# Low-rank rows opened in the projections, first units side by side, the norm's root ahead of the middle work

## The chip, the cores and the metric

The kernel runs on one core of one Trainium2 chip. The metric is the device time of one execution in microseconds (us), the median of several runs. Lower is better.

## The reference

Two transformer blocks follow one another, over 1024 tokens of width 1024, all in float32. Cut to what matters here:

```python
# first block
h = rmsnorm(x, norm_mix);  proj = h @ w_in            # 51 tiles of 128 columns
y_a = retention(rq, rk, rv, rg) @ w_ret_o
y_b = nsa(q, kc, vc, ks, vs, kw, vw, gates) @ w_nsa_o
x = x + (sigmoid(ga) * y_a + sigmoid(gb) * y_b) @ w_out
x = x + conv_ffn(rmsnorm(x, norm_ffn));  x = rmsnorm(x) * norm_final
# second block (ada = silu(c) @ w_ada + b_ada gives shifts, scales and gates)
z, u = split(modulate(rms_norm(x)) @ w_in_2)           # 14 tiles of z, 4 of u
z = z + mu_shift * (z_prev - z)
r, k, v, w_lo, a_lo, g_lo = split(z)                   # 4, 4, 4, 1/2, 1/2, 1 tiles
decay = exp(-exp(-softplus(-(w0 + tanh(w_lo) @ w2)) - 0.5))
a = sigmoid(a0 + a_lo @ a2);  g = sigmoid(g_lo) @ g2
y = rwkv7 recurrence(r, decay, k, v, -kk, kk * a) * g
x = x + gate * concat(y, s5(u)) @ w_out_2
x = x + gate * (silu(h @ w_gate) * (h @ w_up)) @ w_down   # h = modulate(rms_norm(x))
out = rms_norm(x) * final_gain
```

## The kernel before, in words

Activations stay in on-chip memory with the features on the 128 partitions: `xT` is x, `hi` and `lo` are the two parts of the normed x (eight tiles of 128x1024 each). A product `w.T @ h` is made in three passes (high weight by high, high weight by low, low weight by high), so a **unit**, 128 output rows over 1024 tokens, is 8 k tiles times 3 passes times 2 halves = 48 matmuls of 128x512. Weights come by DMA on SP's queue into one of two buffers, are split in two parts (`pool_high` at L192 and a subtraction) and used while the next is loaded. A unit's buffer is split anew for unit u+2 only once unit u's products are done (`products_done`, or `up_done` in the feed-forward), and TensorE starts unit u+2 when that split is done and the accumulator has been read.

The program is a row of stages, each a block of its own per engine with a barrier between (`phase`, L75 and L72). Within a stage every engine runs its list in the order written; waits are on semaphores. `rms_programs` (L294) makes a norm: ACT squares (where no sums are there yet), PE sums over partitions (L343), DVE takes mean and reciprocal (L333, L334), then ACT runs `act_middle`, then the root (L316) and the row's copy (L318), PE spreads the row (L350), and DVE, ACT and POOL make tile after tile of `mid` (L391 or L393), `hi` (L384) and `lo` (L404). In the two feed-forwards `act_middle` is `first_high` (L632: the high parts of the first two weights, which POOL then subtracts at L713); in the last norm it is `gain_too` (L529: four of the eight gains; DVE's scaling at L504 waits for them). `TwoNorms` in the second projections has no such middle work.

Four stages begin with such a norm: the first projections (product at L1409), the first feed-forward (L203), the second projections (L3430) and the second feed-forward (L203). There unit 0 waits at each k tile for that tile of `lo` (`norm.ready`), unit 1 comes whole after it:

```python
for u in range(N):                    # L1399, second projections alike
    for k in range(KD):
        if u == 0:
            norm.ready(pe, k)
```

After the first projections (with retention and compression in them) comes the retention's output product. `SplitTilesAndKeys` (L2005) gives its stage extra work: SP loads the raw keys (two of 64x2x1024, with 18 rows each beside them) and head 0's queries (82x1024), before it loads the stage's weights of units 1 and 2, since the norm's programs are written ahead of the product's. POOL loads two small constants, `edges` and `eye`, waits for both, and only then splits weights. POOL's DMAs go through another queue than SP's.

The second projections make units in the order u (4 tiles), then z tiles 0 to 12, with four S5 gate units in slots 17 to 20, then z tile 13. Tile 12 (`ZLO`) holds the low-rank rows of decay and rate, tile 13 (`ZG`) those of the gate. All z tiles go to DRAM (`proj2T`). The RWKV stage (L2421) then loads both, the low-rank weights `wa2` and `g2`, the chunk mask, the r, k and v of tile 0 and seven small tables on SP's queue; TensorE, ACT and POOL wait for all twelve constants (`CONSTS`), ACT makes tanh (L2944) and sigmoid (L2945) in place, and PE starts with `decay(0)` and `rate(0)` (L2513). ACT's `keys(0)` (L2840) comes behind both and needs the k tile.

## Time and profile before

| what | us |
|---|---|
| median of 3 runs (lowest to highest) | 3860.39 (3858.7 to 3864.57) |
| the profiled execution, its own time | 3864.79 |
| its span | 3863.0 |
| PE busy in the span | 3528.5 (91%) |
| DVE, POOL, ACT busy | 1776.0, 1030.7, 869.9 |

PE is TensorE's matmul sequencer, DVE VectorE, POOL GpSimd, ACT ScalarE, SP the queue that only issues DMAs. Times in rows are microseconds from the span's start. A name such as `ffn_whi` is a buffer of the kernel, its number left out. The granted clock is that of TensorE as a share of 2.4 GHz, so 0.50 is 1.2 GHz. The square brackets behind an instruction say how long its engine had been idle and what ended that. Rows of one instruction kind that follow each other closely are merged, with a count.

### The profile page before, as it was taken

To read this page: it belongs to the slowest core of one execution; us is meant where nothing else is said; L and a number is where in the kernel's file an instruction comes from. 1 tells how busy PE (TensorE), PEld (TensorE's weight loads), DVE (VectorE), ACT (ScalarE), POOL (GpSimd) and SP (SyncE) were. 2 spreads that over 40 slices of the span, in tenths; PEclk is the share of its full clock that TensorE was granted. 3 is DMA by queue.
4 is the path that set the end of the run, shared out by engine and by line. 5 is a ranking of instruction groups with operands and counts; after the bars stand their busy time and mean duration, and the time that the engine had idled before them with its cause. 6 is when DMAs were issued, how large, how long until landed. Compare 5 with 4: busy or idle time off the path is not lost. (4 is left out here: it accounts for less than half of the span.)

```text
span 3863.0 us, 55754 instructions
## 1 busy us (share of the span) xinstructions
PE 3528.5 (91%) x23230; PEld 2909.7 (75%) x23230; DVE 1776.0 (46%) x2725; ACT 869.9 (23%) x1260; POOL 1030.7 (27%) x491
## 2 busy tenths in 40 slices
PE   5999999989999898999999889959896899999997
PEld 4878777767777676888888767748784778888886
DVE  4762555423877734555555636134443322223233
ACT  2012122122434203111111220235431121111112
POOL 3332333333210234121212054122212332122221
PEclk7999999998999998999999989969997899999998
DMA  3453334333000312322222046221002111111111
GB/s 92 137 179 116 110 99 118 104 111 102 8 8 1 113 46 89 109 93 69 72 82 76 30 153 150 89 77 36 19 3 93 55 44 44 55 43 54 38 49 44
DMA packets 310711, 290.79 MB, mean 75 GB/s; under 512 B 21454, under 2 KB 276992, under 8 KB 309304
## 3 DMA queue, kind: packets, MB, share of 16 engines
q1 hardware_dynamic: 283738, 205.62, 18.2%
q10 hardware_dynamic: 26482, 82.06, 5.6%
q8 instruction: 153, 2.51, 0.3%
q0 software_dynamic: 288, 0.20, 0.1%
q14 instruction: 50, 0.41, 0.0%
HBM read 224.26 MB, written 63.57 MB: 75 GB/s over the span
## 5 line engine op out<-in xcount | busy, mean ns | idle before, releaser
L713 POOL TENSOR_TENSOR ffn_wlo<-ffn_raw,ffn_whi 128x1024 fp32r<-128x1024 f32 x88 | 211.4, 2404 | 1067.3 <-ACT ffn_whi L901 1012.9
L203 PE MATMUL up<-h_hi,ffn_whi 128*128 128x512 f32 x1408 | 439.6, 394 | 21.3 <-POOL h_lo L404 20.9
L203 PE MATMUL up<-h_lo,ffn_whi 128*128 128x512 f32 x1408 | 436.2, 391 | 0.0
L203 PE MATMUL up<-h_hi,ffn_wlo 128*128 128x512 f32 x1408 | 435.4, 390 | 0.0
L192 POOL TENSOR_TENSOR whi<-raw,ones 128x1024 fp32r<-128x1024 f32 (+1 forms) x83 | 155.3, 1872 | 754.9 <-PE acc L1409 460.9
L203 PEld LDWEIGHTS up<-h_hi,ffn_whi 128*128 128x128 f32 x1408 | 263.4, 189 | 79.2 <-POOL h_lo L404 14.4
L203 PEld LDWEIGHTS up<-h_lo,ffn_whi 128*128 128x128 f32 x1408 | 265.9, 189 | 56.2
L203 PEld LDWEIGHTS up<-h_hi,ffn_wlo 128*128 128x128 f32 x1408 | 265.7, 189 | 56.1
L1409 PE MATMUL acc<-h_hi,whi 128*128 128x512 f32 x816 | 273.6, 417 | 8.3 <-POOL h_lo L404 8.3
L804 DVE TENSOR_TENSOR ffn_prod<-ffn_act,up 128x1024 f32<-128x1024 f32 x44 | 53.8, 1222 | 465.6 <-PE up L203 460.8
L1409 PE MATMUL acc<-h_lo,whi 128*128 128x512 f32 x816 | 256.6, 396 | 0.0
L1409 PE MATMUL acc<-h_hi,wlo 128*128 128x512 f32 x816 | 254.5, 393 | 0.0
L901 ACT ACTIVATE ffn_whi<-ffn_raw 128x1024 fp32r<-128x1024 f32 x84 | 89.1, 1061 | 633.5 <-PE up L203 581.9
L203 PE MATMUL dn<-ffn_ghi,ffn_dhi 128*128 128x512 f32 x704 | 219.7, 394 | 7.9 <-issue 3.9
L203 PE MATMUL dn<-ffn_ghi,ffn_dlo 128*128 128x512 f32 x704 | 218.5, 392 | 0.0
L203 PE MATMUL dn<-ffn_glo,ffn_dhi 128*128 128x512 f32 x704 | 218.5, 392 | 0.0
L1409 PEld LDWEIGHTS acc<-h_lo,whi 128*128 128x128 f32 x816 | 156.2, 191 | 34.5
L1409 PEld LDWEIGHTS acc<-h_hi,wlo 128*128 128x128 f32 x816 | 155.2, 190 | 34.5
L1409 PEld LDWEIGHTS acc<-h_hi,whi 128*128 128x128 f32 x816 | 150.4, 193 | 39.3 <-issue 6.7
L835 DVE SCALAR_TENSOR_TENSOR xT<-dn,prm,xT 128x1024 f32<-128x1024 f32 x88 | 113.0, 1284 | 124.2 <-PE dn L203 124.2
L811 DVE TENSOR_TENSOR ffn_glo<-ffn_prod,ffn_ghi 128x1024 fp32r<-128x1024 f32 x44 | 139.5, 3170 | 56.7 <-ACT ffn_ghi L925 56.7
L833 DVE TENSOR_TENSOR xT<-xT,dn 128x1024 f32<-128x1024 f32 x88 | 107.4, 1221 | 123.1 <-PE dn L203 123.1
(549 smaller groups left out, 6635.7 us busy)
## 6 DMA issues: line engine op xcount, KB each, us to landing
raw<-w_in SPq DMA_DIRECT2D x51, 512.0 KB
projT<-proj_stage ACTq DMA_DIRECT2D x51, 512.0 KB, 2.7
ffn_ada_raw<-w_ada SPq DMA_DIRECT2D x24, 1024.0 KB, 5.0
ffn_raw<-w_up SPq DMA_DIRECT2D x44, 512.0 KB
ffn_draw<-w_down SPq DMA_DIRECT2D x11, 1024.0 KB, 6.9
ffn_raw<-ffn_w_gate SPq DMA_DIRECT2D x22, 512.0 KB
ffn_raw<-ffn_w_up SPq DMA_DIRECT2D x22, 512.0 KB
ffn_draw<-ffn_w_down SPq DMA_DIRECT2D x11, 1024.0 KB, 4.7
```

The lines of the kernel that those rows point to most:

```text
L192: return nc.gpsimd.tensor_tensor(out, x, one.unsqueeze(2).broadcast_to(x.shape), ALU.mult)
L203: last = nc.tensor.matmul(acc[:, t, :], w[:, k, w_cols], x[:, k, t * HALF:(t + 1) * HALF], start=(k == 0 and i == 0), stop=(k == k_tiles - ...
L713: nc.gpsimd.tensor_tensor(w_lo[i][:], raw[i][:], w_hi[i][:], ALU.subtract).then_inc(s[f"up_split{i}"], 1)
L804: nc.vector.tensor_tensor(prod[j][:].rearrange("p (h t) -> p h t", h=NH), act_out[:].rearrange("p (h t) -> p h t", h=NH), acc[1][:], ALU.m ...
L811: nc.vector.tensor_tensor(g_lo[:, j, :], prod[j][:], g_hi[:, j, :], ALU.subtract).then_inc(s["g_split"], 1)
L833: nc.vector.tensor_tensor(x, x, dn[b][:], ALU.add).then_inc(s[f"down_read{b}"], 1)
L835: nc.vector.scalar_tensor_tensor(out=x, in0=dn[b][:], scalar=prm[:, gate + n:gate + n + 1], in1=x, op0=ALU.mult, op1=ALU.add).then_inc(s[f ...
L901: nc.scalar.activation(w_hi[i][:], raw[i][:], ACT.Copy).then_inc(s[f"up_hi{i}"], 1)
L1409: last = nc.tensor.matmul(acc[b][:, t, :], w[:, k, :], x[:, k, t * HALF:(t + 1) * HALF], start=(k == 0 and i == 0), stop=(k == KD - 1 and ...
```

## The change

Five edits:

- In the four stages that begin with a norm, TensorE's first two units are made side by side: per k tile it waits once and makes 12 matmuls, six for each unit, in place of six. In the first projections the S5 parameters' transposes (`turn_params`), which stood inside unit 1, come after both units.
- In `rms_programs` the root and the row's copy come ahead of `act_middle`.
- The loads of keys and of head 0's queries go from SP's queue to POOL's, ahead of `edges` and `eye`.
- The second projections make `ZLO` and `ZG` in slots 4 and 5, into buffers that the RWKV stage keeps (`lora`, `glo`). ACT applies tanh and sigmoid in slots 6 and 7, behind those units' stores. Eight constants of the RWKV stage are loaded on SP's queue in the last slot.
- The RWKV stage loads only the chunk mask and `sel` (which count as its constants), then r, k and v. PE starts `decay(0)` at once and waits for the constants behind `norms_row(0)`; ACT's tanh and sigmoid and their wait are gone. `krow` has another address.

```diff
@@ rms_programs, ACT
-        if act_middle:
-            act_middle(act)
         act.wait_ge(s["norm_step"], 2)
         nc.scalar.activation(compact[:], compact[:], ACT.Sqrt).then_inc(s["root_done"], 1)
         act.wait_ge(s["root_turned"], 1)
         nc.scalar.activation(row[:], tot[0:NT, 1, 0:P], ACT.Copy).then_inc(s["row_done"], 1)
+        if act_middle:
+            act_middle(act)
@@ feed_forward, PE (both kinds)
+            def first_up_products():
+                for i in range(2):
+                    pe.wait_ge(s[f"up_split{i}"], 1)
+                for k in range(KD):
+                    norm.ready(pe, k)
+                    for i in range(2):
+                        last = tile_products(nc, acc[i], w_hi[i], w_lo[i], hi, lo, k, KD)
+                        if k == KD - 1:
+                            last.then_inc(s[f"up_done{i}"], 1)
...
-            up_products(0, 0)
+            first_up_products()
             up_products(0, 1)
@@ projections_and_retention, PE
+            for b in range(2):
+                pe.wait_ge(s[f"weight_split{b}"], 1)
+            for k in range(KD):
+                norm.ready(pe, k)
+                for b in range(2):
+                    last = tile_products(nc, acc[b], w_hi[b], w_lo[b], hi, lo, k, KD)
+                    if k == KD - 1:
+                        last.then_inc(s[f"products_done{b}"], 1)
+            turn_params()
+            for u in range(2, N):
@@ SplitTilesAndKeys.programs
-        @block.sync
-        def _(sp):
+        @block.gpsimd
+        def _(pool):
             for j, t in enumerate((KS, KW)):
                 k = projT[t * P:(t + 1) * P, :].rearrange("(g d) t -> d g t", d=NSA_D)
-                sp.dma_start(raw[j][low], k).then_inc(s["keys_in"], 16)
-                sp.dma_start(raw[j][NSA_D:rows], ins[("k_krows", "k_wrows")[j]]).then_inc(s["keys_in"], 16)
-            load_queries(nc, sp, N["qh"][0], projT, self.selT, ins, 0, s["query_in"])
-
-        @block.gpsimd
-        def _(pool):
+                pool.dma_start(raw[j][low], k).then_inc(s["keys_in"], 16)
+                pool.dma_start(raw[j][NSA_D:rows], ins[("k_krows", "k_wrows")[j]]).then_inc(s["keys_in"], 16)
+            load_queries(nc, pool, N["qh"][0], projT, self.selT, ins, 0, s["query_in"])
             pool.dma_start(N["edges"][:], ins["k_edges"]).then_inc(s["edges_in"], 16)
             pool.dma_start(N["eye"][:], ins["k_ident"]).then_inc(s["edges_in"], 16)
             pool.wait_ge(s["edges_in"], 32)
@@ projections2_and_s5
-    units = list(range(UU, N_PROJ2)) + list(range(UU))
+    units = list(range(UU, N_PROJ2)) + [ZLO, ZG] + list(range(ZLO))
+    opened = {ZLO: rw["lora"], ZG: rw["glo"]}
... SP
+                if u == N - 1:
+                    sp.wait_ge(s["gelu_done"], NG)
+                    load_rwkv_constants(sp, rw, ins, s["rw_consts"])
+                    sp.wait_ge(s["rw_consts"], 16 * 8)
... ACT (slots 6 and 7); the unit's copy and DVE's shift write opened.get(t, stage[b])
+            def open_low_rank(u):
+                unit_stored(act, u)
+                x, rows, kind = (rw["lora"], slice(0, 64), ACT.Tanh) if units[u] == ZLO else (rw["glo"], slice(0, P), ACT.Sigmoid)
+                nc.scalar.activation(x[rows, :], x[rows, :], kind).then_inc(s[f"opened{u % 2}"], 1)
@@ rwkv, SP
-            sp.dma_start(lora[:], zT[ZLO * P:(ZLO + 1) * P, :]).then_inc(c, 16)
-            sp.dma_start(glo[:], zT[ZG * P:(ZG + 1) * P, :]).then_inc(c, 16)
-            sp.dma_start(wa2[0:64, :], ins["rw_w2_2"].rearrange("a k n -> (a k) n")).then_inc(c, 16)
-            sp.dma_start(wa2[64:128, :], ins["rw_a2_2"].rearrange("a k n -> (a k) n")).then_inc(c, 16)
             sp.dma_start(chunk_mask[:], ins["k_chunk"]).then_inc(c, 16)
+            sp.dma_start(sel[:], ins["k_sel"]).then_inc(c, 16)
... (seven loads behind r, k and v of f == 0 gone)
-        CONSTS = 16 * 12
+        CONSTS = 16 * 2
@@ rwkv, PE
-            pe.wait_ge(s["lora_ready"], 2)
-            pe.wait_ge(s["const_in"], CONSTS)
             decay(0)
             rate(0)
             norms(0)
             norms_row(0)
+            pe.wait_ge(s["const_in"], CONSTS)
             unit(0)
@@ rwkv, ACT
-            act.wait_ge(s["const_in"], CONSTS)
             act.wait_ge(s["consts_done"], 1)
-            nc.scalar.activation(lora[0:64, :], lora[0:64, :], ACT.Tanh).then_inc(s["lora_ready"], 1)
-            nc.scalar.activation(glo[:], glo[:], ACT.Sigmoid).then_inc(s["lora_ready"], 1)
             decay(0)
```

`tile_products` is the body of `three_pass` for one k tile. The second projections' PE loop changes as that of the first, without `turn_params`.

## Rows read from the trace of the kernel before

**Rows 1.** Windows, first projections: us, engines' busy (x), granted clock, DMA share, GB/s.
```profile
63.20:68.46 5.26, 5.26 (x12) 4.10 (x13) 2.95 (x3) 2.11 (x2) 5.12 (x3) 0.50 0.00 0
...
81.88:86.23 4.35, 4.35 (x27) 3.53 (x26) 1.12 (x4) 1.86 (x3) 4.26 (x2) 1.00 0.29 121
```

**Rows 2.** Timeline, first projections: start us, us, what [idle before <-releaser].
```profile
53.46 0.21 ACT L316 ACTIVATE norm_mix_compact<-norm_mix_compact 128x8 f32<-128x8 f32 x1 [4.37 <-DVE norm_mix_compact L334]
...
94.00 0.60 ACT L1435 ACTIVATE proj_stage<-acc 128x512 f32<-128x512 f32 x1 [3.18 <-PE acc L1409]
```

**Rows 3.** Timeline, first feed-forward.
```profile
1448.25 0.20 DVE L334 RECIPROCAL norm_ffn_compact<-norm_ffn_compact 128x8 f32<-128x8 f32 x1
...
1453.05 0.21 ACT L316 ACTIVATE norm_ffn_compact<-norm_ffn_compact 128x8 f32<-128x8 f32 x1
...
1462.80 1.19 PE L203 MATMUL up<-h_hi,ffn_whi 128*128 128x512 f32 x2 [4.97 <-POOL h_lo L404]
...
1481.36 1.34 DVE L797 TENSOR_SCALAR ffn_conv<-up,prm 128x1024 f32<-128x1024 f32 x1 [5.30 <-PE up L203]
```

**Rows 4.** Timeline, second projections.
```profile
2268.67 1.03 DVE L3534 COPY proj_stage<-acc 128x512 f32<-128x512 f32 x1
...
2275.09 1.11 ACT L3454 ACTIVATE proj_stage<-acc 128x512 f32<-128x512 f32 x1 [9.75 <-PE acc L3430]
```

**Rows 5.** Timeline, second feed-forward.
```profile
3074.83 0.20 DVE L334 RECIPROCAL norm_ffn_compact<-norm_ffn_compact 128x8 f32<-128x8 f32 x1
...
3077.18 0.19 ACT L316 ACTIVATE norm_ffn_compact<-norm_ffn_compact 128x8 f32<-128x8 f32 x1
...
3088.12 1.19 PE L203 MATMUL up<-h_hi,ffn_whi 128*128 128x512 f32 x2 [6.19 <-POOL h_lo L404]
...
3110.94 1.06 ACT L901 ACTIVATE ffn_whi<-ffn_raw 128x1024 fp32r<-128x1024 f32 x1 [4.84 <-PE up L203]
...
3113.31 1.03 ACT L918 ACTIVATE ffn_act<-up 128x1024 f32<-128x1024 f32 x1
```

**Rows 6.** Timeline, last norm.
```profile
3829.71 4.26 ACT L529 ACTIVATE xT<-xT,prm 128x1024 f32<-128x1024 f32 x4 [2.33 <-PEq L75]
...
3833.23 0.20 DVE L334 RECIPROCAL final_compact<-final_compact 128x8 f32<-128x8 f32 x1
...
3840.09 9.14 DVE L504 TENSOR_TENSOR xT<-xT,tot 128x1024 f32<-128x1024 f32 x8 [6.66 <-PE tot L350]
```

**Rows 7.** Timeline of PE, a gap in the retention units.
```profile
600.27 0.70 PE L1259 MATMUL tot<-ret_vn,ret_p 128*128 128x256 f32 x2 [2.36 <-ACT ret_kn L1449]
```

**Rows 8.** Windows, just behind that gap.
```profile
601.00:604.20 3.20, 3.20 (x9) 2.54 (x8) 1.32 (x5) 0.00 (x0) 0.00 (x0) 0.50 0.60 238
```

**Rows 9.** Timeline, start of the RWKV stage.
```profile
2546.76 0.34 SPq L2483 DMA_DIRECT2D rw_lora<-proj2T  x1
...
2550.41 0.44 SPq L2495 DMA_DIRECT2D rw_v<-proj2T  x1
...
2564.66 6.62 PE L2513 MATMUL W<-rw_lora,rw_wa 64*128 64x512 f32 x8 [22.82 <-ACT rw_glo L2945]
...
2571.91 1.14 ACT L2840 ACTIVATE rw_kk<-rw_k,rw_neg_k 128x1024 f32<-128x1024 f32 x1
```

**Rows 10.** DMA issues of the RWKV start: KB each, us from issue to landing.
```profile
rw_lora<-proj2T SPq DMA_DIRECT2D x1, 512.0 KB, 3.9
...
rw_v<-proj2T SPq DMA_DIRECT2D x1, 512.0 KB, 8.7
```

**Rows 11.** Timeline, start of the retention output product.
```profile
833.10 3.41 POOL L192 TENSOR_TENSOR whi<-raw,ones 128x1024 fp32r<-128x1024 f32 x1 [12.26 <-DMA raw<-w_ret_o]
...
840.91 1.22 PE L203 MATMUL acc<-h_hi,whi 128*128 128x512 f32 x2 [5.99 <-POOL wlo L171]
```

**Rows 12.** DMA issues of 815 to 842 us.
```profile
nsa_edges<-k_edges POOLq DMA_DIRECT2D x1, 128.0 KB, 5.9
```

**Rows 13.** Groups of instructions, 819 to 829 us.
```profile
L1981 DVE TENSOR_TENSOR h_lo<-ret_Y,h_hi 128x1024 fp32r<-128x1024 f32 x8 | 9.2, 1220 | 5.4 <-ACT h_hi L1975 5.4
```

More of the change, by code:

```diff
@@ L200, in three_pass, with tile_products @@
             ready(k)
-        for i, (w, x) in enumerate(((w_hi, hi), (w_hi, lo), (w_lo, hi))):
-            for t in range(NH):
-                last = nc.tensor.matmul(acc[:, t, :], w[:, k, w_cols], x[:, k, t * HALF:(t + 1) * HALF],
-                                        start=(k == 0 and i == 0), stop=(k == k_tiles - 1 and i == 2))
+        last = tile_products(nc, acc, w_hi, w_lo, hi, lo, k, k_tiles, w_cols)
+    return last
+def tile_products(nc, acc, w_hi, w_lo, hi, lo, k, k_tiles, w_cols=slice(0, P)):
+    for i, (w, x) in enumerate(((w_hi, hi), (w_hi, lo), (w_lo, hi))):
+        for t in range(NH):
+            last = nc.tensor.matmul(acc[:, t, :], w[:, k, w_cols], x[:, k, t * HALF:(t + 1) * HALF],
+                                    start=(k == 0 and i == 0), stop=(k == k_tiles - 1 and i == 2))
     return last
@@ L729, in up_products @@
                     pe.wait_ge(s["b_read" if i else "a_read" if kind == "conv" else "activated"], 2 * c + j)
-                    ready = (lambda k: norm.ready(pe, k)) if first else None
-                    first.clear()
-                    three_pass(nc, acc[i], w_hi[i], w_lo[i], hi, lo, KD, ready=ready).then_inc(s[f"up_done{i}"], 1)
+                    three_pass(nc, acc[i], w_hi[i], w_lo[i], hi, lo, KD).then_inc(s[f"up_done{i}"], 1)
             def down_products(d):
@@ L1397, in attention_part @@
                     turn_values(u - TURN_V)
-            for u in range(N):
+            for b in range(2):
[8 more added lines that the diff above has]
+            for u in range(2, N):
                 b, m = u % 2, u - START
                 pe.wait_ge(s[f"weight_split{b}"], u // 2 + 1)
-                if u >= 2:
-                    pe.wait_ge(s[f"acc_read{b}"], u // 2)
+                pe.wait_ge(s[f"acc_read{b}"], u // 2)
                 for k in range(KD):
-                    if u == 0:
-                        norm.ready(pe, k)
-                    for i, (w, x) in enumerate(((w_hi[b], hi), (w_hi[b], lo), (w_lo[b], hi))):
-                        for t in range(NH):
-                            last = nc.tensor.matmul(acc[b][:, t, :], w[:, k, :], x[:, k, t * HALF:(t + 1) * HALF],
-                                                    start=(k == 0 and i == 0), stop=(k == KD - 1 and i == 2))
-                    if k == 1 and u == 1:
-                        turn_params()
+                    last = tile_products(nc, acc[b], w_hi[b], w_lo[b], hi, lo, k, KD)
                     if k == 1 and 0 < u - QUARTER <= 4:
@@ L3415, in gate_spread @@
                 last.then_inc(s["gate_spread"], 1)
-            for u in range(N):
+            for b in range(2):
+                pe.wait_ge(s[f"weight_split{b}"], 1)
+            for k in range(KD):
+                norm.ready(pe, k)
+                for b in range(2):
+                    last = tile_products(nc, acc[b], w_hi[b], w_lo[b], hi, lo, k, KD)
+                    if k == KD - 1:
+                        last.then_inc(s[f"products_done{b}"], 1)
+            for u in range(2, N):
                 b, n = u % 2, tiles_of(u)
                 pe.wait_ge(s[f"weight_split{b}"], u // 2 + 1)
-                if u >= 2:
-                    pe.wait_ge(s[f"acc_read{b}"], u // 2)
+                pe.wait_ge(s[f"acc_read{b}"], u // 2)
                 if u == GLU_SLOT:
@@ L3425, in _ @@
                 for k in range(n):
-                    if u == 0:
-                        norm.ready(pe, k)
-                    for i, (w, x) in enumerate(((w_hi[b], x_hi), (w_hi[b], x_lo), (w_lo[b], x_hi))):
-                        for t in range(NH):
-                            last = nc.tensor.matmul(acc[b][:, t, :], w[:, k, :], x[:, k, t * HALF:(t + 1) * HALF],
-                                                    start=(k == 0 and i == 0), stop=(k == n - 1 and i == 2))
+                    last = tile_products(nc, acc[b], w_hi[b], w_lo[b], x_hi, x_lo, k, n)
                     if k == n - 1:
@@ L3458, in store @@
                         act.wait_ge(s["rest_done"], 1)
-                    nc.scalar.activation(stage[b][:].rearrange("p (h t) -> p h t", h=NH), acc[b][:], ACT.Identity,
+                    dst = opened.get(t, stage[b])[:]
+                    nc.scalar.activation(dst.rearrange("p (h t) -> p h t", h=NH), acc[b][:], ACT.Identity,
                                          scale=rest[:, t:t + 1]).then_inc(s[f"acc_half{b}"], 1)
@@ L3537, in read @@
                     mu = PRM["mu_shift_2"] + t
[L3538 removed]
+                    z = opened.get(t, stage[b])
+                    nc.vector.scalar_tensor_tensor(out=z[:, 1:S], in0=x[:, 0:S - 1], scalar=prm[:, mu:mu + 1], in1=z[:, 1:S],
                                                    op0=ALU.mult, op1=ALU.add).then_inc(s[f"acc_read{b}"], 1)
```

57 lines of the change are left out of this document (30 added, 27 removed).

## The prediction, made before the changed kernel was run

> **What bounds the kernel now.** I read the page first: TensorE is busy almost throughout, so only stretches where it stands or runs at 1.2 GHz can give time. The list of waits named them, and the timelines of the stages' starts showed what each hangs on. Four stages start on a norm whose `lo` tiles POOL makes one by one; TensorE makes six matmuls per tile and waits for the next [rows 1 to 5]. In both feed-forwards the norm itself waits: DVE has the reciprocal ready, and ACT's root starts 4.6 us later in the one, 2.15 us later in the other, behind the weights' high parts [rows 3, 5]. The last norm has that too [rows 6]. The largest wait of all is the RWKV start, 22.8 us until tanh and sigmoid are done [rows 9]. At the retention's output TensorE stands 6.0 us for POOL's split of unit 1 [rows 11].
>
> **The RWKV start.** Twelve constants, tanh and sigmoid leave the path. SP issues its first load at 2546.8, the first product starts at 2564.7 and ACT's keys at 2571.9 [rows 9], so decay and rate take 7.3 us, and keys follow without a wait. After the change the products can start at 2546.8, so the keys' floor is 2554.1: a gain of 17.8. But keys need r, k and v. Before, v lands at 2550.4 + 8.7 = 2559.1, with 3328 KB moved up to it; the first 512 KB land 3.9 us after their issue, the other 2816 KB by 8.4 us later, 335 KB/us [rows 9, 10]. Now mask, `sel`, r, k and v are 2112 KB: 3.9 + 1600/335 = 8.7 us, so 2555.5, and the gain is **16.4**. At worst v lands as before: 12.8. Moved work: tanh and sigmoid go to slots 6 and 7 (each a pass of 1.1 us, as L901's, and a table load, the 1.3 us that lie between L901's end and Silu [rows 5]) of the projections, where ACT idles 9.75 us per unit [rows 4]; their wait for the unit's store stands just ahead of a wait for the same store in the next unit's copy, so it queues nothing new. Eight loads in the last slot sit on SP behind the last weight, under two units; nothing on SP is behind them. Cost 0; without that cover, 2.4 us twice.
>
> **The root.** First feed-forward: reciprocal done 1448.45, root at 1453.05 [rows 3], gain **4.6**. The table load doesn't come back: in the first stage ACT idles 4.37 us directly ahead of the root, so its table was loaded ahead of the wait [rows 2]; if it did, 1.3 less. `first_high` now runs under the spread of the row by TensorE, and POOL's two subtractions behind it under the first `mid` and `hi`. They end about when that `hi` is there, so here POOL is late next, by little if at all. Second: 3075.03 against 3077.18, **2.1** [rows 5]. Last norm: four gains, 4.26 us in all, end at 3833.97 [rows 6]; with a table load of 1.3 the root comes at 3835.3 and DVE at 3840.1, 4.8 later. Now the root comes at 3833.45, the spread is done at 3838.3, and the gains start behind root, transpose and row. These take about 1 us (an estimate: most of the 4.8 are the 16 matmuls of the spread), so the gains end at 3838.7 and are late next: **1.4**.
>
> **Side by side.** Shared terms: the first 12 matmuls at 1.2 GHz take 5.26 us [rows 1]; a unit at 2.4 GHz takes the 9.75 us that ACT idles between two units' copies and the 1.1 us of one copy, 10.9 us or 0.227 per matmul [rows 4], so the other 84 take 19.0. In the cold start TensorE falls more than two `lo` tiles behind POOL and, at 2.7 us per tile from there, doesn't wait for the norm again. But both units now end together, and unit 2's split starts only then.
> - First projections: start 63.2, unit 0 ends 86.1, POOL's split 4.35 [rows 1] and two semaphores, unit 2 at 90.7. Before it was 93.9 [rows 2]. Gain 3.2; gap of 2.0 us behind `turn_params`. DVE's and ACT's S5 work, queued behind `turn_params`, starts 3.5 us later; it waits for units' copies in each of the next units, which covers that.
> - First feed-forward, on the old clock of events: start 1462.8, unit 0 ends 1485.7, unit 1 1487.1; DVE must make three passes of 1.34 us before accumulator 0 is free [rows 3], so unit 2 starts at 1489.8 and not at 1481.3 + 10.9 = 1492.2. Gain 2.4, gap 2.7.
> - Second projections: unit 0 ends at 2264.2, as before (9.75 + 1.1 ahead of the copy at 2275.1), unit 1 1.4 us later, but DVE reads accumulator 0 only at 2268.7 to 2269.7, behind its second norm. Unit 2 starts at 2269.8, not at 2275.0 [rows 4]. Gain 5.2, gap 4.3.
> - Second feed-forward, old clock of events: start 3088.1, unit 0 ends 3111.0, unit 1 3112.4. ACT needs 3.4 us from unit 0's end (3110.9) to the end of Silu (3114.3) [rows 5], so unit 2 starts at 3114.8. Before, 3110.9 + 10.9 = 3121.8. Gain 7.0, gap 2.4.
>
> The gaps have a price. A gap of 2.36 us in the retention was followed by 3.2 us at granted clock 0.50, 1.2 GHz [rows 7, 8]: half of it, 1.6 us, is lost. Gaps of that size or more cost 1.6 each here, the 2.0 us one half of that: net **2.4, 0.8, 3.6 and 5.4**.
>
> **Keys on POOL's queue.** Moved past SP's two weight loads: four key loads of 1312 KB together and 328 KB of queries; put ahead of POOL's `edges` and `eye`, and POOL waits for these before it splits unit 1's weight. SP's weight now starts at once; before, POOL got it at 833.1 [rows 11]. Which lands last? Assume that both queues get a packet in turn and a packet is one row: 666 rows of keys, queries and constants on 16 engines are 42 each, which go with 42 of the 64 of the weight (1024 rows of 512 bytes). So `edges` land after about 1.64 + 0.19 + 0.34 = 2.2 MB; before, the weight landed behind 1.64 + 0.19 + 0.5 = 2.3. That is the same moment, near 833. I take **0**. Best: the whole 6.0 us gap and the cold 5.3 us behind it go, 6.0 + 2.6 = +8.6 [rows 1, 11]. Worst by contention: DVE's eight subtractions keep it busy 9.2 us of this stretch [rows 13], and `edges`, 128 KB, took 5.9 us to land beside them [rows 12]; if the keys only start behind them, POOL gets going about 6.6 us later: -6.6. The Trainium skill (SBUF — State Buffer, SBUF: two separate sides) says that a DMA of the GpSimd queue has its descriptors written by GpSimd, which a VectorE instruction that holds the shared port pair blocks. By that the sum would be 30.1 us; without it, 36.7. The trace agrees so far as a slow landing goes, and shows no more.
>
> **Sum:** 16.4 + 4.6 + 2.1 + 1.4 + 2.4 + 0.8 + 3.6 + 5.4 + 0 = **36.7 us**, against the profiled execution's 3864.8: 3828.1. The median of the runs stands 4.4 us below that execution, so 3860.4 - 36.7 = **3823.7**.
>
> **Rivals.**
> - *The side-by-side units give nothing.* The same product done earlier only waits longer for split and read, and the clock stays low longer behind the gaps. Against it: the split time is plain in [rows 1], and unit 2's start follows from it. Without those 12.2 us: 3835.9. Chance 0.10.
> - *POOL late by the contention above:* 3823.7 + 6.6 = 3830.3. For it: [rows 12, 13]. Chance 0.14.
> - *POOL's wait for edges is over before the weights:* the gap goes, 3815.1. For it: SP's weights are first. Chance 0.12.
> - *Slower: POOL's queue moves bytes slowly whatever stands beside it.* Place: POOL's wait for `edges`. Price by [rows 12]: 128 KB in 5.9 us is 22 KB/us; 1640 + 192 KB take 84 us from 819.6, POOL splits from 904 and not from 833, +71, so 3823.7 + 71 = 3895. It decides from where `edges` land later than 833 + 37 = 870, below 37 KB/us. Against it: with that load on 16 engines the 5.9 us hold a fixed part and a share lost to SP's queue. Chance 0.04.
> - *The RWKV move hides nothing because z is as late as before:* 3827.3. Inside the range of the forecast.
>
> **How the numbers follow.** Forecast as summed: 0.60. Its own bounds: RWKV 12.8 to 17.8, clock behind four gaps 0 to 2.7 each, the table load. The range reaches to the contention case, the gap-gone case and most of the nothing-gained case: 3810 to 3838, with about 0.2 outside. About 0.2% (7.7 us) is what a measurement of this kernel can tell from no change. All cases but the slow queue lie over 20 us below before; slower 0.04, same 0.02 for several bounds falling badly at once, faster 0.94.
>
> **What would show it.** ACT's keys of tile 0 start within 9 us of the RWKV stage's first issue; no tanh there. The root at L316 follows the reciprocal by under 0.1 us in both feed-forwards. TensorE waits for `h_lo` once per stage, and then a wait of 2 to 4.3 us ahead of unit 2 with clock 0.50 behind it. The wait for L171 stays near 6 us. I am wrong if unit 2's wait is over 5 us, if POOL's first split in the retention output starts after 840, or if ACT's keys still wait past 2559.

## The result, and the profile after

| | before | changed |
|---|---|---|
| median of the runs | 3862.48 us (4 runs, 3858.7 to 3866.29) | 3832.15 us (4 runs, 3822.89 to 3834.68) |
| profiled execution | 3864.8 us, span 3863.0 | 3830.97 us, span 3829.2 |
| mean granted clock | 0.946 | 0.945 |

The changed kernel takes 0.9916 of the time of before (95% interval 0.9897 to 0.9934). That is 30.3 us by the medians, where 36.7 were forecast: 3832.15 against 3823.7, inside the range of 3810 to 3838, and in the forecast case.

The chain of TensorE's waits, laid over that of before, shows where the two spans part. A negative number is time gained within the stretch; the stretches are bounded by waits of TensorE that both kernels have (2952.58 is where its wait for L171 in the second output product begins), and they sum to the 33.8 us between the spans.

| stretch (us of before) | change, us | edited there |
|---|---|---|
| up to 63.20 | -1.05 | no |
| 63.20 to 238.42, first projections | -1.82 | side by side |
| 238.42 to 821.46 | -4.86 | no |
| 821.46 to 925.35, retention output | +1.84 | keys on POOL's queue |
| 925.35 to 1444.46 | -2.53 | no |
| 1444.46 to 1462.80, norm | -4.57 | root |
| 1462.80 to 2182.19, first feed-forward | -1.99 | side by side |
| 2182.19 to 2241.19 | -0.59 | no |
| 2241.19 to 2538.88, second projections | -1.84 | side by side |
| 2538.88 to 2581.05, RWKV start | -15.02 | RWKV |
| 2581.05 to 2952.58, the rest of RWKV | +6.16 | no |
| 2952.58 to 3071.05, second output product | +2.90 | no |
| 3071.05 to 3088.12, norm | -2.07 | root |
| 3088.12 to 3800.16, second feed-forward | -5.35 | side by side |
| 3800.16 to 3829.73 | -1.21 | no |
| from 3829.73, last norm | -1.80 | root |

The edited stretches give 32.6 us. The others move too, by up to 6 us either way, and that had to be understood before any part could be judged.

The RWKV start, timeline of all engines of the changed kernel, answering to [rows 9] (start, duration, engine, line, operation, count, idle before and its releaser):

```profile
2530.19 0.33 SPq L2508 DMA_DIRECT2D rw_mask<-k_chunk  x1
...
2530.24 3.75 PE L2527 MATMUL W<-rw_lora,rw_wa 64*128 64x512 f32 x4 [5.00 <-PEq L75]
...
2531.98 0.43 SPq L2517 DMA_DIRECT2D rw_v<-proj2T  x1
...
2539.46 1.15 ACT L2853 ACTIVATE rw_kk<-rw_k,rw_neg_k 128x1024 f32<-128x1024 f32 x1 [0.55 <-DMA rw_v<-proj2T]
```

TensorE starts with the stage's first issue. The keys start 9.3 us after it (25.1 before). ACT waits 0.55 us for v just ahead of them; v landed 7.5 us behind its own issue.

The norm of the first feed-forward, answering to the root's rows of [rows 3]:

```profile
1439.82 0.20 DVE L340 RECIPROCAL norm_ffn_compact<-norm_ffn_compact 128x8 f32<-128x8 f32 x1
1440.06 0.21 ACT L320 ACTIVATE norm_ffn_compact<-norm_ffn_compact 128x8 f32<-128x8 f32 x1 [2.78 <-DVE norm_ffn_compact L340]
...
1440.91 1.04 ACT L638 ACTIVATE ffn_whi<-ffn_raw 128x1024 fp32r<-128x1024 f32 x1
...
1442.10 4.65 POOL L719 TENSOR_TENSOR ffn_wlo<-ffn_raw,ffn_whi 128x1024 fp32r<-128x1024 f32 x2 [27.78 <-ACT ffn_whi L638]
...
1447.32 4.68 POOL L410 TENSOR_TENSOR h_lo<-norm_ffn_mid,h_hi 128x1024 fp32r<-128x1024 f32 x2 [0.57 <-ACT h_hi L390]
```

The root runs 0.04 us after the reciprocal. POOL has both low parts of the weights done 0.57 us before the first `hi` is there, so the moved `first_high` makes nothing late.

Unit 2 of the four stages in TensorE's timeline (the wait stands at the end), and the windows of 4 us behind the four gaps, whose last three columns are granted clock, DMA share and GB/s:

```profile
89.22 0.73 PE L209 MATMUL acc<-h_hi,whi 128*128 128x512 f32 x2 [1.84 <-POOL wlo L1226]
...
1477.28 0.70 PE L209 MATMUL up<-h_hi,ffn_whi 128*128 128x512 f32 x2 [2.81 <-DVE ffn_conv L812]
...
2254.07 1.14 PE L209 MATMUL acc<-h_hi,proj_whi 128*128 128x512 f32 x2 [4.23 <-DVE proj_stage L3559]
...
3089.02 0.73 PE L209 MATMUL up<-h_hi,ffn_whi 128*128 128x512 f32 x2 [2.34 <-POOL ffn_wlo L719]
```

```profile
89.22:93.22 4.00, 4.00 (x11) 3.19 (x12) 3.93 (x5) 1.50 (x2) 3.92 (x2) 0.61 0.54 133
1477.28:1481.28 4.00, 4.00 (x18) 3.32 (x19) 1.22 (x1) 3.59 (x4) 0.62 (x1) 1.00 0.45 135
2254.07:2258.07 4.00, 4.00 (x11) 3.18 (x12) 1.07 (x1) 1.08 (x1) 3.09 (x2) 0.57 0.93 319
3089.02:3093.02 4.00, 4.00 (x12) 3.20 (x13) 2.82 (x2) 1.80 (x2) 2.38 (x1) 0.67 0.45 131
```

The gaps were forecast at 2.0, 2.7, 4.3 and 2.4 us. The first three have the releasers that were forecast. In the second feed-forward ACT's Silu was to be last; it ends at 3088.82, and POOL's split, at 3088.96, releases TensorE. The clock is low behind three of the gaps, and full, all 4 us, behind the one of 2.81.

The retention output, answering to [rows 11], and the second output product, which nobody edited:

```profile
811.34 28.20 SPq L159 DMA_DIRECT2D raw<-w_ret_o  x4
...
816.34 0.56 POOL L2044 DMA_DIRECT2D nsa_eye<-k_ident  x1
...
827.21 3.28 POOL L192 TENSOR_TENSOR whi<-raw,ones 128x1024 fp32r<-128x1024 f32 x1 [10.31 <-DMA nsa_eye<-k_ident]
...
834.89 1.22 PE L209 MATMUL acc<-h_hi,whi 128*128 128x512 f32 x2 [8.39 <-POOL wlo L171]
...
2933.00 27.52 SPq L159 DMA_DIRECT2D raw<-w_out  x4
...
2943.66 1.89 POOL L192 TENSOR_TENSOR whi<-raw,ones 128x1024 fp32r<-128x1024 f32 x1 [11.71 <-DMA raw<-w_out]
...
2948.90 1.22 PE L209 MATMUL acc<-h_hi,whi 128*128 128x512 f32 x2 [22.59 <-POOL wlo L171]
```

In the first, POOL no longer waits for a weight but for `eye`, which it issued itself, ninth and last, 5.0 us after the weight's issue. The split starts 15.9 us after the stage's first issue; before, 14.0. In the second the first weight took 10.7 us to land; the same load took 5.3 us before.

What the queues moved in the retention output, in the first 4 us behind the weight's issue and in the 2 us after them (`q1` is SP's queue, `q0` POOL's; packets, MB, busy share):

```profile
q1 hardware_dynamic: 1675, 0.85, 70.2%
```

```profile
q0 software_dynamic: 107, 0.44, 77.9%
q1 hardware_dynamic: 404, 0.20, 35.0%
```

POOL issued its first load at 811.88. None of its packets moved before 815.7, 3.8 us later, and by then most of SP's two weights (2048 rows of 512 bytes) had gone. In the five kernels with the keys on POOL's queue the delay is 3.3 to 3.8 us.

### The profile page after: what moved, and what is told of

The parts are those of the page before. It is cut to its first block and busy times, and to the rows that moved or that the text cites. A ratio compares the mean times of both kernels' runs of the same rounds, so it can differ in the third digit from the quotient of the medians.

```text
span 3829.2 us, 55751 instructions
## 1 busy us (share of the span) xinstructions
PE 3526.1 (92%) x23230; PEld 2914.4 (76%) x23230; DVE 1777.9 (46%) x2725; ACT 870.1 (23%) x1261; POOL 1037.2 (27%) x498
## 5 line engine op out<-in xcount | busy, mean ns | idle before, releaser
L209 PE MATMUL up<-h_hi,ffn_whi 128*128 128x512 f32 x1408 | 438.9, 393 | 16.4 <-POOL h_lo L410 11.2
L209 PE MATMUL acc<-h_hi,whi 128*128 128x512 f32 x1136 | 374.1, 411 | 51.3 <-POOL wlo L171 32.1
L209 PE MATMUL acc<-h_lo,whi 128*128 128x512 f32 x1136 | 358.2, 397 | 0.0
L209 PE MATMUL acc<-h_hi,wlo 128*128 128x512 f32 x1136 | 355.7, 395 | 0.0
L209 PEld LDWEIGHTS acc<-h_hi,whi 128*128 128x128 f32 x1136 | 211.6, 193 | 96.7 <-POOL wlo L171 34.6
L209 PEld LDWEIGHTS acc<-h_lo,whi 128*128 128x128 f32 x1136 | 217.7, 192 | 47.6
L209 PEld LDWEIGHTS acc<-h_hi,wlo 128*128 128x128 f32 x1136 | 217.4, 191 | 47.9
```

Of the source, the lines that this page charges most:

```text
L209: last = nc.tensor.matmul(acc[:, t, :], w[:, k, w_cols], x[:, k, t * HALF:(t + 1) * HALF], start=(k == 0 and i == 0), stop=(k == k_tiles - ...
```

## The experiments

a2 to a4 and c2 to c4 are the kernel before with some parts of the change, as the diff ahead of the prediction has them; the others are the changed kernel with the edit shown.

| kernel | median us (runs) | ratio to before | span |
|---|---|---|---|
| a1, keys on SP again | 3830.34 (6) | 0.9910 (0.9892 to 0.9929) | 3828.9 |
| a2, side by side alone | 3851.46 (12) | 0.9972 (0.9959 to 0.9985) | 3848.0 |
| a3, RWKV part alone | 3846.76 (7) | 0.9954 (0.9935 to 0.9973) | 3829.5 |
| a4, root alone | 3855.86 (12) | 0.9976 (0.9963 to 0.9989) | 3849.5 |
| b1, two waits moved | 3823.44 (4) | 0.9896 (0.9866 to 0.9926) | 3823.4 |
| b2, staggered units | 3820.83 (4) | 0.9884 (0.9854 to 0.9913) | 3816.2 |
| b3, b1 and b2 | 3811.26 (4) | 0.9864 (0.9838 to 0.9891) | 3806.5 |
| b4, the changed kernel again | 3829.92 (4) | 0.9904 (0.9876 to 0.9931) | 3838.7 |
| c1, b3 with keys on SP | 3817.11 (4) | 0.9879 (0.9857 to 0.9900) | 3810.9 |
| c2, RWKV and root | 3839.85 (1) | | 3838.0 |
| c3, RWKV and side by side | 3827.29 (1) | | 3825.5 |
| c4, side by side and root | 3838.43 (1) | | 3836.7 |

### b4: what two executions of one program differ by

> The changed kernel once more, unedited, to see what differs between two executions. Theory 1 (the wait of 22.6 us ahead of the second output product, and the 6.4 us lost between 2600 and 2915 us, are chance): the wait is 16.3 us this time, or another value, and the stretch of the RWKV stage takes another time. Rival (they belong to this program): the wait is again 22.6 or 28.1 us, and the stretch is 315.4 us long again, from the wait for the keys' root of tile 1 to the last y_squared. Median of the runs 3829 to 3835.

The RWKV stretch was as long again (377.86 us for 377.69 between the two waits used below), which alone would speak for the rival. But the stretch of 238.42 to 821.46, with no edit in it, took 583.04 us before, 578.18 in the changed kernel and 583.77 in the same kernel again. The rest of the RWKV stage, cut by the same two waits in every kernel, tells most. Its windows in the kernel before, the changed one, a3 and b1 (columns: window, length, busy time of PE, PEld, DVE, ACT, POOL with counts, granted clock, DMA share, GB/s):

```profile
2581.05:2952.58 371.53, 324.88 (x8096) 282.39 (x8096) 149.45 (x302) 140.00 (x257) 86.32 (x61) 0.90 0.05 16
```

```profile
2548.62:2926.31 377.69, 330.44 (x8096) 287.92 (x8096) 149.50 (x302) 139.94 (x257) 86.40 (x61) 0.89 0.05 15
```

```profile
2553.05:2919.94 366.89, 320.13 (x8096) 277.20 (x8096) 149.15 (x302) 139.99 (x257) 86.40 (x61) 0.93 0.05 16
```

```profile
2542.14:2921.81 379.67, 330.47 (x8096) 287.64 (x8096) 149.22 (x302) 140.14 (x257) 86.37 (x61) 0.90 0.05 15
```

The same 8096 matmuls, DVE, ACT and POOL busy to within 0.4 us, and between 366.9 and 379.7 us, most of the difference in TensorE's busy time and the shortest at the highest clock. In all 14 profiled executions the stretch lies between these two, with the RWKV part and without it (without: 371.5, 371.9, 377.3, 378.5). The ten with it average 374.9 us, the four without 374.8. So the 6.2 us "lost" there lie within what kernels without the RWKV part show too, and are not put down to it. For the wait at the second output product the rival holds: 24.0 us, far from 16.3.

### a2: the side-by-side units alone

> The kernel before with the side-by-side units of the four stages alone. Theory 1 (the parts add, each gap of over 2.3 us behind them costs about 1.6 us of low clock): 12.2 us faster than before; unit 2 starts 27.1 us after the first product in the first projections, 27.5 in the first feed-forward, 28.4 in the second projections, 26.3 in the second feed-forward, as in the changed kernel. Rival 1 (it gives nothing in time, since the low clock behind the gaps eats it): 0 to 4 us. Rival 2 (the parts do not add, the clock falls where it falls): between 6 and 18 us, and the granted clock's mean differs from 0.946.

11 us by the ratio, 10.0 by the medians, so Rival 1 falls. Rival 2 is not excluded: its range holds 10 and 11 too, and the profiled execution's mean clock is 0.953, though the clocks of the other executions, of this kernel and of the one before, spread as far (0.943 to 0.954). Unit 2 starts 27.9, 27.4, 28.4 and 26.6 us after the first product, the first of these 0.8 us later than expected. The gaps are 1.84, 2.81, 4.23 and 2.34 us again. The stretches of the four stages, bounded as in the table above:

| | first projections | first ffn | second projections | second ffn |
|---|---|---|---|---|
| before | 175.22 | 719.39 | 297.69 | 712.04 |
| changed | 173.40 | 717.40 | 295.85 | 706.69 |
| a2 | 172.58 | 717.20 | 295.50 | 705.29 |

Its windows behind the four gaps give the price of the clock:

```profile
90.25:94.25 4.00, 4.00 (x17) 3.30 (x18) 3.93 (x5) 1.50 (x2) 3.92 (x2) 1.00 0.56 137
1486.05:1490.05 4.00, 4.00 (x18) 3.29 (x19) 1.22 (x1) 3.59 (x4) 0.62 (x1) 1.00 0.46 134
2263.05:2267.05 4.00, 4.00 (x11) 3.19 (x12) 1.07 (x1) 1.08 (x1) 3.10 (x2) 0.60 0.92 318
3107.28:3111.28 4.00, 4.00 (x18) 3.31 (x19) 2.81 (x2) 1.80 (x2) 2.40 (x1) 1.00 0.45 131
```

Here the clock stayed full behind the first and the last gap, and these stages are 0.8 and 1.4 us shorter than in the changed kernel, where it fell. That is the price forecast (half of 1.6, and 1.6); whether it is paid changes from one execution to the next (b1, with the clock full behind the first gap, took 172.75 us there, and c3, with it full behind the last, 705.14).

### a3: the RWKV part alone

> The kernel before with the low-rank rows made early and kept, the constants loaded early and the shorter start of the RWKV stage, alone. Theory 1 (it gives what the start shows and the rest of the stage is the same): keys start 9.3 us after the first issue instead of 25.1, the kernel is 15.9 us faster. In the changed kernel's profile 6.4 us of this were lost inside the stage with the same waits, and 6.3 at the start of the second mixer's output product, where the first weight landed 10.7 us after its issue instead of 5.3. Theory 2 (both losses come with this part, systematically): 3 to 10 us faster, and the weight again lands over 9 us after its issue. Theory 1 says that the weight's landing and the clock are chance of one execution: then 15 to 17 us.

17.8 us by the ratio (interval 10 to 25), 14.7 by the medians. The start gained 15.9 us (2538.88 to 2581.05 of before), the weight landed as before, and TensorE waited 16.2 us for it: Theory 1, as far as this part alone goes. Over the ten executions with this part the start's gain is 14.9 to 16.6 us.

### a4: the root alone

> The kernel before with the norm's root and row copy ahead of ACT's other work, alone. Theory 1 (the parts add): 4.6 in the first feed-forward, 2.1 in the second, 1.4 to 1.8 in the last norm, together 8.1 to 8.5 us faster; root within 0.1 us of the reciprocal. Rival (high parts of the weights are late now, so POOL's split of the first weights and the first lo wait): TensorE's wait for the first h_lo grows from 5.0 and 6.2 us and the gain is under 5 us.

The stretches: 13.78 us for 18.34 in the first feed-forward's norm, 14.99 for 17.07 in the second's; from the last norm's start to the end 31.65 for 33.27. Together 8.3 us; the ratio says 9.3, the medians 5.6. The last of the three is not all the root's: from the last norm to the end the ten executions with this part took 30.3 to 32.9 us, the four without 32.3 to 33.3. The rows of the norm itself are steadier: from the reciprocal's start to DVE's scaling it is 5.5 us in all ten and 6.8 to 6.9 in the four, 1.4 us less. The wait for the first `lo` stays 4.98 and 6.20 (4.97 and 6.19 before): the rival falls.

### a1 and c1: keys back on SP's queue

```
-        @block.gpsimd
-        def _(pool):
+        @block.sync
+        def _(sp):
             for j, t in enumerate((KS, KW)):
...
-            load_queries(nc, pool, N["qh"][0], projT, self.selT, ins, 0, s["query_in"])
+            load_queries(nc, sp, N["qh"][0], projT, self.selT, ins, 0, s["query_in"])
```

> The changed kernel with the keys' and queries' loads back on SP's queue, all else as changed. The two traces: in the changed kernel POOL's first split of the retention output starts 15.9 us after the stage's first issue and waits for eye on POOL's queue, before it was 14.0 us and waited for the weight; TensorE's gap for L171 is 8.4 us, before 6.0. Theory 1 (that part costs, by the wait for edges and eye behind the keys): the gap is 6.0 again, the first split comes 14.0 us after the first issue, and the kernel is 1.8 to 2.4 us faster than the changed one, some 32.5 us faster than the one before. Rival (the queue makes no difference, the longer gap is the stage's start falling otherwise): the gap stays near 8.4 and the time is that of the changed kernel, 30.3 us below before.

The gap is 6.5 us, 5.99 to 7.20 in all nine kernels that have the keys on SP's queue; it is 8.39, 7.76 and 8.02 in the three executions with the keys on POOL's and its wait for `eye` in place. From the first product to the attention's start (821.46 to 925.35) that is 103.1 to 104.3 us against 105.7, 104.8 and 103.9. The means are 103.6 and 104.8 us, so the moved loads cost about 1.2 us; the times of whole kernels can't tell (3830.34 against 3829.92 and 3832.15).

### b1: two waits moved

```
             pool.dma_start(N["eye"][:], ins["k_ident"]).then_inc(s["edges_in"], 16)
-            pool.wait_ge(s["edges_in"], 32)
...
     def pool_part(self, pool):
         N, s = self.N, self.s
+        pool.wait_ge(s["edges_in"], 32)
...
             act.dma_start(zz[:], self.gated).then_inc(s["gated_in"], 16)
+            act.wait_ge(s["weight_loaded0"], 16)
             for i in range(2):
```

> The changed kernel with two waits moved: in the retention output POOL waits for edges and eye only at its fifth unit, where it first needs the queries, and in the second mixer's output product ACT's two loads of x (4 MB) wait until the first weight has landed. Theory 1 (the split of the retention output waited for eye, 1.8 us behind the weight's landing): TensorE's gap for L171 there falls from 8.4 to 6.5 or less. Rival (the weight itself lands later, since the keys on the other queue take its bandwidth): POOL's first split still starts 15.9 us after the first issue and the gap stays 8.4. Theory 2 (in the second output product the weight's 512-byte packets took turns with the 4 MB of x): the wait for L171 is 16.2 to 16.5 us, as in the kernel before, in place of 22.6 and 28.1, and the wait at tile 4 is near 4.5. Rival: the gated tiles alone hold it up, and the wait stays over 20.

In the retention output (timeline of b1):

```profile
815.67 26.14 SPq L159 DMA_DIRECT2D raw<-w_ret_o  x4
...
821.23 1.92 POOL L192 TENSOR_TENSOR whi<-raw,ones 128x1024 fp32r<-128x1024 f32 x1
823.24 3.25 POOL L171 TENSOR_TENSOR wlo<-raw,whi 128x1024 fp32r<-128x1024 f32 x1
827.62 0.73 PE L209 MATMUL acc<-h_hi,whi 128*128 128x512 f32 x2 [1.65 <-DVE h_lo L1994]
```

The weight was there 5.6 us or less after its issue. The wait for L171, 8.4 us, is gone. Theory 1 holds (6.5 or less was expected) and its rival falls, but the weight had not landed 1.8 us ahead of `eye`, as Theory 1 reasoned: it was there some 10 us ahead. The stretch takes 96.7 us and not 105.7. The prediction had this as its rival "the gap goes", at 8.6 us; 9.0 were measured. The weight was there in time for it, and one wait of POOL's stood in front.

The early split has a price. DVE's eight subtractions of `h_lo`, in the changed kernel and in b1 (shortest, median and longest in ns):

```profile
L1994 DVE TENSOR_TENSOR h_lo<-ret_Y,h_hi x8: 1218/1219/1226, 812.5 to 820.4; 128x1024 fp32r<-128x1024 f32 x8
```

```profile
L1994 DVE TENSOR_TENSOR h_lo<-ret_Y,h_hi x8: 1210/1217/4051, 816.8 to 829.8; 128x1024 fp32r<-128x1024 f32 x8
```

In b1 POOL's split runs among them (821.2 to 826.5). They take 14.2 us in all instead of 9.2, the longest 4.05 us instead of 1.2, and TensorE waits 1.65 us for one of them, the row at 827.62. b3 shows the same (14.2 us, a wait of 1.66). POOL's own subtraction takes 3.25 us there, and 2.34 us in the second output product below.

In the second output product (timeline of b1):

```profile
2928.51 9.89 SPq L159 DMA_DIRECT2D raw<-w_out  x3
...
2933.65 0.81 ACTq L3667 DMA_DIRECT2D xT<-xsave  x2
2933.70 1.89 POOL L192 TENSOR_TENSOR whi<-raw,ones 128x1024 fp32r<-128x1024 f32 x1 [6.24 <-DMA raw<-w_out]
2935.67 2.34 POOL L171 TENSOR_TENSOR wlo<-raw,whi 128x1024 fp32r<-128x1024 f32 x1
...
2938.06 1.22 PE L209 MATMUL acc<-h_hi,whi 128*128 128x512 f32 x2 [16.25 <-POOL wlo L171]
```

The weight is back at 5.1 us, as Theory 2 had it. The worth is less than the wait suggests: from the first issue to the next norm the stage takes 111.85 us here, 111.78 before and 114.7 in the changed kernel, 2.9 us more and not 6.3, since TensorE waits at tile 4 for the gated tiles in any case (1.5 and 4.5 us before, 2.6 in the changed kernel).

### b2: unit 0 ends first

```
+def first_two(both):
+    return [(k, b) for k in range(both) for b in range(2)] + [(k, b) for b in range(2) for k in range(both, KD)]
...
-                for k in range(KD):
-                    norm.ready(pe, k)
-                    for i in range(2):
-                        last = tile_products(...)
+                for k, i in first_two(5 if w_ada is not None else 6):
+                    if i == 0:
+                        norm.ready(pe, k)
+                    last = tile_products(...)
```

The first projections and the first feed-forward use 5, the second projections and the second feed-forward 6. In the norm of the second projections:

```
                                               in1=both_rstd, op0=ALU.mult, op1=ALU.mult).then_inc(s["mid_done"], 1)
-            dve.wait_ge(s["mid_done"], KD)
-            dve.wait_ge(s["rstd_done"], 2)
-            for k in range(KD):
-                nc.vector.scalar_tensor_tensor(out=xT[:, k, :], ...)
+                if k >= 2:
+                    first_normed(k - 2)
+            for k in (KD - 2, KD - 1):
+                first_normed(k)
```

where `first_normed(k)` waits for `mid_done` k + 1 and `rstd_done` 2 and makes the same pass.

> The changed kernel in which the first two units run side by side only for the first 5 tiles (6 in the second projections and the second feed-forward) and then unit 0 is finished ahead of unit 1; and in the second projections DVE makes each first-normed tile of x between two of its mids instead of all eight behind them. Theory 1 (the gaps ahead of unit 2 exist because both units end together, and in the second projections because DVE is late): gaps 1.84, 2.81, 4.23, 2.34 become 0, under 0.5, under 0.5 and under 1.5; unit 2 starts 1.8, 2.7, 4, 1.1 us earlier after the stage's first product, 9.6 us in all, and 1.6 more for each gap whose low clock goes: 8 to 15 us faster than the changed kernel. Rival (a later wait takes its place: unit 3 waits for unit 1's split as unit 2 did): the waits reappear ahead of unit 3 and the time is within 3 us of the changed kernel.

The gaps of 1.84 and 2.81 are gone, 4.23 became 1.82 (under 0.5 was expected) and now waits for POOL's split of unit 2, 2.34 became 1.01. The four stages take 170.26, 713.25, 291.41 and 704.73 us: 3.1, 4.2, 4.4 and 2.0 less than in the changed kernel. Over the three kernels with this edit (b2, b3, c1) against the seven executions with both units ending together the means differ by 3.3, 3.1, 2.8 and 1.6. In the second projections the share of the order of units and that of DVE's order are not separated. By the medians the kernel is 9 to 11 us faster than the changed one. The rival falls; in two stages a smaller wait did take the place.

### b3: both

> Both of the kernels above in one. Theory 1: their gains add, some 10 to 20 us below the changed kernel, 3812 to 3822 against a kernel before at 3862. Rival (the clock falls elsewhere instead and takes it back): within 5 us of the changed kernel, with a mean granted clock of under 0.945.

3811.26 us, 19 to 21 below the changed kernel, 1.4% below before: the fastest version found. The gains stand where b1 and b2 had them, retention output 96.7 us, second output product 111.7, the four stages 170.1, 714.6, 292.6 and 704.7. In c1, the same with the keys on SP:

> The kernel of b3 with the keys' and queries' loads on SP's queue ahead of the weights, as in the kernel before. Theory 1 (with POOL's wait for edges and eye out of the way, the order of the loads decides: SP's weight lands 5.6 us after the stage's first issue when the keys are on POOL's queue and 14.0 us when they are ahead of it): TensorE waits 5.9 to 6.8 us for L171 in the retention output as in the kernel before, and the stretch from the first product there to the attention's start is some 9 us longer than b3's 96.7. Rival (the weight's landing is bound by the bytes of all queues together): POOL splits early here too, no gap, and the time is b3's.

```profile
811.41 22.57 SPq L159 DMA_DIRECT2D raw<-w_ret_o  x4
...
821.66 3.28 POOL L192 TENSOR_TENSOR whi<-raw,ones 128x1024 fp32r<-128x1024 f32 x1 [12.39 <-DMA raw<-w_ret_o]
...
829.34 1.22 PE L213 MATMUL acc<-h_hi,whi 128*128 128x512 f32 x2 [6.59 <-POOL wlo L171]
```

The weight, issued 3.9 us late behind the keys, keeps POOL waiting 14.2 us from the stage's first issue, TensorE waits 6.6 us and the stretch takes 103.3 us. That is 6.6 longer than b3's; 9 were expected. The intervals of c1 and b3 overlap, so this rests on the rows.

### c2 to c4: which parts make the weight late

> The kernel before with the RWKV part and the root part. Which edits make the first weight of the second output product land late? It waited 16.2 to 16.4 us for L171 in before and with one part alone, 22.6 to 28.1 in all four executions of kernels with the three parts together. Theory 1 (a program's own timing or chance, no part): either value. Theory 2 (it takes the RWKV part with a second one): 22 to 28 here and in the next. Time 3834 to 3840 in all by the sum of the parts.

> The kernel before with the RWKV part and the side-by-side units. By Theory 2 of c2 the wait for L171 at the second output product is 22 to 28 us; by Theory 1 either. Time by the sum of the parts 3862 - 16 - 11 = 3835.

> The kernel before with the side-by-side units and the root part, no RWKV part. By Theory 2 of c2 the wait at the second output product is 16.2 to 16.4 us; by Theory 1 either. Time by the sum of the parts 3862 - 11 - 8.5 = 3842.

The wait at the second output product is 16.4, 16.6 and 16.2 us: Theory 2 falls. The wait was long in the four executions that have all three parts and x's loads at once (22.6, 24.0, 28.1, 27.5), short in the seven that lack a part, and short in the three with x's loads behind the weight. In the first 5 us SP's queue moved 0.60 to 0.69 MB in all of these, late or not.

What lateness costs can be read from the queues. In the changed kernel, from 5.5 to 10.5 us behind the weight's issue (`q1` is SP's queue, `q10` ACT's; packets, MB, busy share), and in the kernel before over the same time:

```profile
q10 hardware_dynamic: 143, 2.08, 97.2%
q1 hardware_dynamic: 144, 0.07, 4.8%
```

```profile
q10 hardware_dynamic: 142, 2.06, 96.4%
q1 hardware_dynamic: 143, 0.07, 4.8%
```

Once both queues have work, they move the same number of packets, SP's of 512 bytes and ACT's of 14.5 KB on average. One packet of each on 16 engines then takes 0.56 us (an estimate: 5 us for 143 pairs on 16 engines). By this estimate a weight that still lacks some ten packets on one engine when ACT's large ones begin would land 5.5 us late, as in the changed kernel; that it was so is not shown. Why a few of its packets are left in some executions and not in others stays open. That x's 4 MB have a part in it rests on three short waits (b1, b3, c1) against four long ones; the seven other executions had x's loads at once too, and a short wait.

Times of the single runs: 3839.85, 3827.29 and 3838.43, where 3834 to 3840, 3835 and 3842 were expected; c3 is off by 8, which is the spread of single runs (a3's seven lie between 3831.33 and 3854.10).

## Why the prediction was right, and where it was off

One pair of executions is a poor measure of a part. The means over all 14 profiled executions, with the number of executions that have the part and that lack it (the side-by-side rows leave out b2, b3 and c1, whose units are staggered, and the row of the keys leaves out b1 and b3, where POOL's wait is moved):

| part | forecast | changed against before | means of all | executions |
|---|---|---|---|---|
| RWKV start | 16.4 | 15.0 | 15.8 | 10 and 4 |
| root, first feed-forward | 4.6 | 4.6 | 4.4 | 10 and 4 |
| root, second feed-forward | 2.1 | 2.1 | 2.1 | 10 and 4 |
| root, last norm | 1.4 | 1.8 | 1.4, by the rows in a4 | 10 and 4 |
| side by side, first projections | 2.4 | 1.8 | 1.9 | 7 and 4 |
| side by side, first feed-forward | 0.8 | 2.0 | 1.7 | 7 and 4 |
| side by side, second projections | 3.6 | 1.8 | 3.2 | 7 and 4 |
| side by side, second feed-forward | 5.4 | 5.35 | 5.9 | 7 and 4 |
| keys on POOL's queue | 0 | -1.8 | -1.2 | 3 and 9 |
| weight late, second output product | none | -2.9 | -2.8 | 4 and 10 |

**The RWKV start.** Keys came 9.3 us after the first issue and not 8.7. The step itself held: v's landing sets them.

**The root.** All three terms held. In the last norm the four gains on ACT are late next, as forecast (DVE waits for L535 and not for TensorE).

**Side by side**, 12.2 forecast: 11.0 in this execution, 12.7 by the means. The four gaps were right to 0.2 us. One term was off: in the first feed-forward the low clock was charged behind a gap of 2.7 and came in none of the seven executions. In the second projections unit 2 starts 5.3 us earlier, as forecast, and the stretch gained only 1.8. The wait for `s_u<-uperm`, 2.81 us here and 0.95 before, fills the difference in this pair, but it doesn't belong to the side-by-side units: it is 1.65, 2.01 and 3.06 us in a3, c2 and a4, which lack them, and 2.05 to 2.81 in the seven that have them. Most of the shortfall is the spread of this stretch, which took 296.3 to 300.2 us in the four executions without the units and 293.9 to 296.1 in the seven with them.

**Keys on POOL's queue**, 0: it cost about 1.2 us, and the term came near by luck, since the reasoning behind it did not hold. It took both queues to move packets from the start, so that the weight and `edges` would land at the same moment. But POOL's queue moved its first packet 3.8 us behind POOL's first issue, 4.3 us behind the weight's, and the weight, first on its own queue, was there after 5.6 us. `eye` landed 15.9 us after the first issue, of which 5.0 are POOL issuing nine loads one after the other. That each issue takes POOL 0.5 to 0.8 us was not in the sum, though the two issues of POOL's in that stretch of the kernel before would have told it:

```profile
819.59 0.72 POOL L2033 DMA_DIRECT2D nsa_edges<-k_edges  x1 [12.61 <-POOLq L75]
820.30 0.53 POOL L2034 DMA_DIRECT2D nsa_eye<-k_ident  x1
```

That queues take turns packet by packet, however long the packets, is not what failed: the two queues at the second output product did so, 143 packets against 144. That POOL's loads would only start behind DVE's subtractions did not come either: they started to move at 815.7, amid subtractions that ran from 812.5 to 821.6. The prediction priced that case at 6.6 us and put beside it a rule of the Trainium skill (SBUF — State Buffer, SBUF: two separate sides), that VectorE holding the shared port pair blocks the GpSimd queue's descriptors. The section says it of VectorE's 2-port modes; an instruction with two inputs in SBUF, as these subtractions are, holds the pair only against a GpSimd instruction that reads SBUF. The trace agrees with that half: in b1, beside POOL's split, the longest subtraction took 4.05 us instead of 1.2. POOL's loads landed 7.3 to 10.8 us after their issues; what of that is their late start and what the shared bandwidth, no run here separates.

**The sum.** By the means the parts give 32.4 us for 36.7 forecast, against 30.3 by the medians (25 to 40 by the interval). The largest miss is the late weight, 2.8 us, which the prediction had not looked for; then the keys, 1.2, and the RWKV start, 0.6. The three parts alone give 11, 18 and 9 us by their ratios, 38 together, each with some 5 to 7 us of interval to either side, so they agree with the sum and can't refine it. The rival "nothing from side by side" is refuted by a2, the slow queue by b1 and by the profile, and the signs forecast for the root (under 0.1 us), for `h_lo` (one wait per stage) and for the RWKV stage (no tanh) are in the traces. Four signs were missed: the keys came at 9.3 us where "within 9" was said, the wait for L171 was 8.4 where "near 6" was said, the first gap was 1.84 where at least 2 was said, and the clock did not fall behind the gap of 2.81.

## What to carry to other kernels

When loads are moved to an engine's own queue, look at what that engine waits for next: here a wait for two small constants that nobody needed for four more units hid a gain of 9 us. When units are interleaved to cover a slow producer, let one of them end first, so that its buffers and its split come free under the other. And judge a part by the stretch between two waits that both kernels share, since whole executions of one program differ here by more than most parts are worth.

## What was not expected of the hardware

- The clock behind a gap does not go by the gap's length alone. In seven executions with the same four gaps, the 4 us behind 4.23 us were at 0.57 to 0.61 every time, those behind 2.81 us at 1.00 every time, those behind 1.84 and 2.34 us low five times in seven each.
- Two queues with work shared by packets and not by bytes: 144 of 512 bytes against 143 of 14.5 KB on average in the same 5 us. A 512 KB load of 512-byte rows landed 5.1 to 5.5 us or 10.7 to 15.8 us after its issue beside the same 6.5 MB on ACT's queue, with as many bytes moved in the first 5 us.
- Loads issued by POOL cost it 0.5 to 0.8 us each, and the first packet moved 3.3 to 3.8 us behind the first issue; SP's first packets there moved about 1 us behind theirs.
- A pass of DVE with two inputs and POOL's split slow each other: 4.05 us for 1.2 on DVE, 3.25 for 2.34 on POOL in b1.
- Unedited stretches of one program differ by 5.6 us in 580 between two executions, 5.5 us of it in TensorE's busy time, at a granted clock of 0.98 and 0.97.
